# A SwiGLU gate/up projection by seven block products in place of eight, with the sums of weight blocks on GpSimd

## The reference

```python
h = rms_norm(x, ffn_pre_g[l])                      # (512, 1024)
f = silu(h @ w_gate[l]) * (h @ w_up[l])            # w_gate, w_up: (1024, 2816)
f = f @ w_down[l]                                  # w_down: (2816, 1024)
x = x + rms_norm(f, ffn_post_g[l])
```

## Time and profile before

| | us |
|---|---|
| median of 3 runs | 1101.09 (1100.99 to 1101.46) |
| span of the profiled execution | 1098.9 |
| PE busy | 1081.2 |
| DVE busy | 621.1 |
| ACT busy | 410.0 |
| POOL busy | 5.2 |

### The profile page before, as it was taken

One profiled execution on the slowest core, in us unless ns is written; L12 is line 12 of the kernel. 1 busy time (PEld: TensorE's weight loads), 2 busy tenths in 40 slices (PEclk: granted clock), 3 DMA queues, 4 the chain that ended last, 5 costly groups with the idle time before them and its releaser, 6 DMA issues.

```text
span 1098.9 us, 16669 instructions
## 1 busy us (share of the span) xinstructions
PE 1081.2 (98%) x6662; PEld 656.5 (60%) x6662; DVE 621.1 (57%) x1419; ACT 410.0 (37%) x810; POOL 5.2 (0%) x18
## 2 busy tenths in 40 slices
PE   8999999999999999999999999999999999999997
PEld 5887894695444444444488888748744444444443
DVE  6998998973432433322579889898633433422014
ACT  5636355553332332221244464456532322331000
POOL 1000000000000000000000000000000000000000
PEclk9999999999999999999999999999999999999999
DMA  8513212254324323323023150134623323232001
GB/s 310 172 56 102 92 40 97 96 166 142 115 77 153 109 83 115 114 79 115 1 79 115 40 151 5 43 111 154 183 86 115 116 96 115 91 101 77 1 20 58
DMA packets 58173, 109.64 MB, mean 100 GB/s; under 512 B 7025, under 2 KB 7281, under 8 KB 57969
## 3 DMA queue, kind: packets, MB, share of 16 engines
q1 hardware_dynamic: 58096, 108.58, 30.8%
HBM read 106.46 MB, written 2.10 MB: 99 GB/s over the span
## 4 chain that ended last, share of the span: by engine, by line
PE 91%; DMA 3%; DVE 3%; ACT 1%; SPq 1%; issue 1%; ACTq 0%; DVEq 0%
PE ps L508 84%; DMA raw<-weights_dram 3%; PE ps L512 3%; PE ps L716 1%; PE ps L700 1%; DVE ring L1158 1%; DMA xs<-x_dram 1%; DVE E L1287 1%; ACT ring L786 0%; PE ps L635 0%; SPq L453 0%; ACT gbc L786 0%; PE ps L677 0%; PE ps L638 0%; PE ps L620 0%
## 5 line engine op out<-in xcount | busy, mean ns | idle before, releaser
L508 PE MATMUL ps<-hT,ring 128*128 128x512 f16 (+1 forms) x3264 | 547.4, 329 | 0.0
L508 PEld LDWEIGHTS ps<-hT,ring 128*128 128x128 f16 x3264 | 319.1, 98 | 221.4
L508 PE MATMUL ps<-ring,U 128*128 128x512 f16 x1440 | 313.4, 379 | 0.0
L1158 DVE SCALAR_TENSOR_TENSOR ring<-raw,ring 128x512 f16<-128x512 f32 x368 | 231.2, 685 | 89.4 <-ACT ring L786 88.7
L786 ACT ACTIVATE ring<-raw 128x512 f16<-128x512 f32 x368 | 208.1, 621 | 126.6 <-PE ps L508 80.4
L508 PEld LDWEIGHTS ps<-ring,U 128*128 128x128 f16 x1440 | 140.8, 98 | 167.2 <-issue 0.3
L1490 DVE SCALAR_TENSOR_TENSOR R<-ps,R 128x512 f32<-128x512 f32 (+1 forms) x52 | 31.7, 609 | 256.2 <-ACT R L961 255.9
L508 PE MATMUL ps<-ring,hT 128*128 128x256 f16 x1152 | 133.3, 273 | 1.4 <-DVE hT L1247 1.3
L961 ACT ACTIVATE R<-ps 128x512 f32<-128x512 f32 (+1 forms) x52 | 27.6, 530 | 276.1 <-PE ps L508 276.0
L508 PEld LDWEIGHTS ps<-ring,hT 128*128 128x128 f16 x1152 | 112.1, 98 | 16.1 <-issue 1.9
L1287 DVE SCALAR_TENSOR_TENSOR E<-E,par 128x256 f32<-128x256 f32 x240 | 102.1, 479 | 0.2
(11 more groups left out here) (109 smaller groups left out, 498.9 us busy)
## 6 DMA issues: line engine op xcount, KB each, us to landing
raw<-weights_dram SPq DMA_DIRECT2D x368, 256.0 KB, 3.3
gbc<-gains_dram SPq DMA_DIRECT2D x8, 512.0 KB, 6.2
xs<-x_dram SPq DMA_DIRECT2D x4, 512.0 KB, 7.0
U<-weights_dram SPq DMA_DIRECT2D x8, 256.0 KB, 7.9
out_dram<-xs SPq DMA_DIRECT2D x8, 256.0 KB, 2.0
cst<-consts_dram SPq DMA_DIRECT2D x1, 1296.0 KB, 12.2
bd<-pool_w_dram SPq DMA_DIRECT2D x8, 16.0 KB, 9.8
par<-params_dram SPq DMA_DIRECT2D x1, 76.0 KB, 6.7
```

Source lines behind the costliest of these rows:

```text
L508: ins = mm(dst, st, mv_, start=first and i == 0, stop=last and i == 2, **kw)
L1158: V.scalar_tensor_tensor(out=ring[:, slot % RING, 1, raw_part(part)], in0=raw_home(n)[0], scalar=W_SCALE, in1=ring[:, slot % RING, 0, raw_ ...
```

## The change

Gate/up slots 5 to 21 (`FAST`) of each layer, 17 in each, are computed by the Strassen-Winograd scheme. Tokens are cut into halves (256 each), the 1024 rows of the sum into halves (512 each), and the 256 columns into gate and up (128 each). Seven products of 512 rows x 128 columns x 256 tokens take the place of eight. Four of them use sums of weight blocks, four use sums of activation blocks, and three sums of products are needed.

- PE: `seven_products`, 7 x 4 x 3 = 84 matmuls of 256 columns for a slot, in four banks: 0 to 3 or 4 to 7 in turn. Between the products it waits for `p1_copied`, `u_sb`, `c12_ps` and `v_sb`. Two matmuls in each of the first two such slots of a layer set the state of two banks.
- ACT: three copies of 128 x 256 out of PSUM for a slot (`p1_copy`, `u_copy`, `v_copy`); in a layer once, four copies of 128 x 1024 of the transposed activations in float32 (`h32_copy`) and four of their sums to float16 (`hS_hi_of`).
- DVE: two additions of 128 x 256 for a slot (`c12_add`, `c22_add`), both with one operand in PSUM; in a layer once, four sums of 128 x 1024 (`h_sums`) and four low halves of that size (`hS_lo_of`).
- POOL: three additions for a slot, of 128 x 1024, 128 x 512 and 128 x 512 float32, with both operands in SBUF, into `xsum`. Each waits for the one before it. The first waits until DVE has split the third chunk of the FAST slot before, the second until it has split the fourth.
- Splits: a FAST slot has 7 blocks of 128 x 512 in place of 4, split in chunks of 1, 2, 2 and 2 blocks. The last two chunks read `xsum`. `raw` has 8 parts in place of 4. The ring has the same size, but is given out in 32 blocks of 128 x 512 (`QUADS`).
- Order: `hidden_steps` becomes `head_steps` (up to slot 3) and `main_steps`, which spreads the chunks of the next slots between the other steps. In `main_steps` one slot is split for each slot multiplied, but where the slots to split are down slots (4 blocks each) there are two: in layer 0 while f = 19, 20 and 21 run; in layer 1 f = 18 has one FAST and one down slot, f = 19 has one slot, and f = 20 and 21 have two.

```diff
-NRAW = 4
+NRAW = 8
 EARLY = 2 * PARTS
-RING = 8
+QUADS = 32
...
+FAST = tuple(range(GU_HEAD + 1, FT))
...
+        xsum = sb("xsum", [P, 4, RAW])
...
+            for n in FAST_SLOTS:
+                base, i = PARTS * n, 3 * FAST_NO[n]
+                r = (base - EARLY) % NRAW
+                if i:
+                    pool.wait_ge(lo_split, PARTS * FAST_SLOTS[i // 3 - 1] + 3)
+                for part in range(3):
+                    _, landed, value = raw_home(base + part)
+                    pool.wait_ge(landed, value)
+                nc.gpsimd.tensor_tensor(xsum[:, 0:2, :], raw[:, r:r + 2, :], raw[:, r + 1:r + 3, :],
+                                        ALU.add).then_inc(x_sum, 1)
+                if i:
+                    pool.wait_ge(lo_split, PARTS * FAST_SLOTS[i // 3 - 1] + 4)
+                pool.wait_ge(x_sum, i + 1)
+                nc.gpsimd.tensor_tensor(xsum[:, 2, :], xsum[:, 0, :], raw[:, r + 2, :], ALU.add).then_inc(x_sum, 1)
+                _, landed, value = raw_home(base + 3)
+                pool.wait_ge(landed, value)
+                pool.wait_ge(x_sum, i + 2)
+                nc.gpsimd.tensor_tensor(xsum[:, 3, :], xsum[:, 2, :], raw[:, r + 3, :], ALU.add).then_inc(x_sum, 1)
...
+            def seven_products(l, f, between):
+                n, i = l * SLOTS + GU0 + f, fast_no(l, f)
+                ba = gu_bank(f)
+                bb, bc, be = ba + 1, ba + 2, ba + 3
+                for b in (ba, bb, bc, be):
+                    take(b, f_sb, fno(l, f, 0))
+                pe.wait_ge(hS_lo, 4 * (l + 1))
+                if f in FAST[0:2]:
+                    for b in (bb, bc):
+                        mm(bank[b][:, 0:HALF], quad(n, 0, 0)[:, 0:P], hT[:, 0, 0, 0:HALF], start=True, stop=True)
+                def product(b, q, a, first, last):
+                    for k in range(KT // 2):
+                        cols = slice(P * k, P * (k + 1))
+                        for j, (pw, pa) in enumerate(((0, 0), (0, 1), (1, 0))):
+                            ins = mm(bank[b][:, 0:HALF], quad(n, q, pw)[:, cols], a[pa][:, k, :],
+                                     start=first and k == 0 and j == 0, stop=last and k == KT // 2 - 1 and j == 2,
+                                     skip_group_check=True)
+                    return ins
+                def whole(j):
+                    return [hT[:, p, KT // 2 * j:KT // 2 * (j + 1), :] for p in range(2)]
+                def h(i, j):
+                    return [w[:, :, half(i)] for w in whole(j)]
+                def hs_(c):
+                    return [hS[c][:, 0], hS[c][:, 1]]
+                product(ba, Q_A11, h(0, 0), True, True).then_inc(p1_ps, 1)
+                between(2)
+                product(be, Q_X1, hs_(0), True, True)
+                between(4)
+                pe.wait_ge(p1_copied, i)
+                product(bb, Q_X3, hs_(1), False, True).then_inc(p6_ps, 1)
+                between(6)
+                product(ba, Q_B21, h(0, 1), False, True)
+                between(9)
+                pe.wait_ge(u_sb, i)
+                product(bb, Q_X2, hs_(2), False, True).then_inc(p7_ps, 1)
+                between(11)
+                pe.wait_ge(c12_ps, i)
+                product(bc, Q_B22, hs_(3), False, True)
+                between(13)
+                pe.wait_ge(v_sb, i)
+                return product(bb, Q_X4, h(1, 1), False, True)
...
+            def h32_copy(l, t):
+                act.wait_ge(h_lo, xno("fpre", l, t) + 1)
+                copy(h32_by_tile[:, t // 2, :, P * (t % 2):P * (t % 2 + 1)],
+                     pair(t).rearrange("p (k t) -> p k t", k=KT), A_SCALE / RN).then_inc(h32_in, 1)
...
+            def p1_copy(l, f):
+                i = fast_no(l, f)
+                act.wait_ge(p1_ps, i)
+                copy(bank[gu_bank(f) + 1][:, 0:HALF], bank[gu_bank(f)][:, 0:HALF]).then_inc(p1_copied, 1)
+            def u_copy(l, f):
+                i = fast_no(l, f)
+                act.wait_ge(p6_ps, i)
+                if i > 1:
+                    act.wait_ge(c12_ps, i - 1)
+                copy(u_w, bank[gu_bank(f) + 1][:, 0:HALF]).then_inc(u_sb, 1)
+            def v_copy(l, f):
+                i = fast_no(l, f)
+                act.wait_ge(p7_ps, i)
+                if i > 1:
+                    act.wait_ge(c22_ps, i - 1)
+                copy(v_w, bank[gu_bank(f) + 1][:, 0:HALF]).then_inc(v_sb, 1)
...
+            def main_steps(l, i0, i1):
+                for i in range(i0, i1):
+                    f, _ = HIDDEN[i]
+                    new = FREED_BY[l * NU + FIRST_OF[GU0] + i - 1] if i > i0 else []
+                    if i > i0:
+                        silu(l, *HIDDEN[i - 1])
+                    split_hi_chunks(new, 0, 2)
+                    if f in FAST:
+                        p1_copy(l, f)
+                    split_hi_chunks(new, 2, 3)
+                    hidden_hi(l, *HIDDEN[i - 1])
+                    if f in FAST:
+                        u_copy(l, f)
+                    split_hi_chunks(new, 3, 4)
+                    if f in FAST:
+                        v_copy(l, f)
+                silu(l, *HIDDEN[i1 - 1])
+                split_hi(*FREED_BY[l * NU + FIRST_OF[GU0] + i1 - 1])
+                hidden_hi(l, *HIDDEN[i1 - 1])
...
+                elif part == 1:
+                    for j in (1, 2):
+                        _, landed, value = raw_home(i + j)
+                        act.wait_ge(landed, value)
+                    copy(quads2(n, Q_B22, 0), raw_pair(i + 1), W_SCALE).then_inc(hi_split, 1)
+                else:
+                    act.wait_ge(x_sum, 3 * FAST_NO[n] + (1 if part == 2 else 3))
+                    copy(quads2(n, Q_X1 if part == 2 else Q_X3, 0), xsum[:, 2 * part - 4:2 * part - 2, :],
+                         W_SCALE).then_inc(hi_split, 1)
...
+                h32_copy(l, 0)
+                h32_copy(l, 1)
                 split_hi(z + 18)
                 square_y("post", l, 3)
-                hidden_steps(l, 0, 1)
+                head_steps(l, 0, 1)
                 split_hi(z + 19)
                 square_x("fpre", l, 3)
-                split_hi(z + 20)
                 h_hi_of("fpre", l, 2)
+                h32_copy(l, 2)
                 h_hi_of("fpre", l, 3)
-                split_hi(z + 21)
-                hidden_steps(l, 1, len(HIDDEN))
-                hidden_hi(l, *HIDDEN[-1])
-                split_hi(*(z + DN0 + c + RING for c in range(N_DN - DN_TAIL)))
+                h32_copy(l, 3)
+                head_steps(l, 1, 5)
+                for c in range(4):
+                    hS_hi_of(l, c)
+                head_steps(l, 5, 2 * GU_HEAD)
+                main_steps(l, 2 * GU_HEAD, len(HIDDEN))
+                split_hi(*REST[l])
...
+            def c12_add(l, f):
+                b = gu_bank(f)
+                dve.wait_ge(u_sb, fast_no(l, f))
+                V.tensor_tensor(bank[b + 2][:, 0:HALF], bank[b + 3][:, 0:HALF], u_w, ALU.add).then_inc(c12_ps, 1)
+            def c22_add(l, f):
+                b = gu_bank(f)
+                dve.wait_ge(v_sb, fast_no(l, f))
+                V.tensor_tensor(bank[b + 3][:, 0:HALF], bank[b + 3][:, 0:HALF], v_w, ALU.add).then_inc(c22_ps, 1)
...
+            def main_steps(l, i0, i1):
+                for i in range(i0, i1):
+                    f, _ = HIDDEN[i]
+                    new = FREED_BY[l * NU + FIRST_OF[GU0] + i - 1] if i > i0 else []
+                    split_lo_chunks(new, 0, 1)
+                    if i > i0:
+                        hidden(l, *HIDDEN[i - 1])
+                    split_lo_chunks(new, 1, 2)
+                    hidden_lo(l, *HIDDEN[i - 1])
+                    if f in FAST:
+                        c12_add(l, f)
+                    split_lo_chunks(new, 2, 3)
+                    if f in FAST:
+                        c22_add(l, f)
+                    split_lo_chunks(new, 3, 4)
+                hidden(l, *HIDDEN[i1 - 1])
+                split_lo(*FREED_BY[l * NU + FIRST_OF[GU0] + i1 - 1])
+                hidden_lo(l, *HIDDEN[i1 - 1])
...
+                head_steps(l, 1, 4)
+                h_sums(l)
+                head_steps(l, 4, 5)
+                for c in range(4):
+                    hS_lo_of(l, c)
+                head_steps(l, 5, 2 * GU_HEAD)
+                main_steps(l, 2 * GU_HEAD, len(HIDDEN))
+                split_lo(*REST[l])
```

More of the change, by code:

```diff
@@ L105, with fast @@
 assert len(UNIT_AT) == NT * SLOTS
+def fast(n):
+    return n % SLOTS - GU0 in FAST
+QUAD0, BEFORE, holder = [], [], {}
+top = 0
+for n in range(L * SLOTS):
+    if fast(n) and any((top + q) % QUADS == QUADS - 1 for q in (1, 3, 5)):
+        top += 1
+    places = [(top + q) % QUADS for q in range(7 if fast(n) else 4)]
+    QUAD0.append(top)
+    BEFORE.append(max([holder[p] for p in places if p in holder], default=-1))
+    for p in places:
+        holder[p] = n
+    top += len(places)
+FAST_SLOTS = [n for n in range(L * SLOTS) if fast(n)]
+FAST_NO = {n: i for i, n in enumerate(FAST_SLOTS)}
```

(44 more changed lines are left out.)

147 lines of the change are left out of this document (104 added, 43 removed).

## The result

The changed kernel takes **1087.41 us** (median of 4 runs, 1085.18 to 1088.65), the kernel before 1101.28 us beside it: a ratio of 0.9871 [0.9857, 0.9885], 13.9 us faster. Forecast were 1088.8 us in a range of 1066 to 1108. The total was near; three of its terms were far off, one of them too dear and two too cheap. The execution that was profiled is the fastest of the four (1085.18 us): its span of 1083.4 us is 15.5 us under the one before, where the medians differ by 13.9 us.

The account below looks back on a forecast made before the run. The prediction took the changed part to be bound by PE. Its terms, -40.4 + 0.9 + 19.9 + 0.4 + 3.9 + 4 - 1 = -12.3 us, took 1101.1 us to 1088.8 us, range 1066 to 1108 us.

Parts of the forecast that it names:

- the term of the slots: In f = 7 to 18 of each layer, PE waits 0.83 us for `c12_ps` per slot: 24 x 0.83 = +19.9 us.
- the head: Handovers between DVE and POOL in each layer's head make slot 5 start 2 us late: +4 us for two layers.
- the places with two slots at once: Four chunks ahead of `p1_copy` cost 0.6 us in five slots; with f = 18 of layer 1, +3.9 us together.
- 84 matmuls for 48, 34 slots: PE's slot falls from 10.36 to 9.17 us, 1.19 us less in each of 34 slots: -40.4 us.
- `p1_copy` in plain slots: PE's restart after ACT's copy loses between 0 and 0.2 us, taken as 0.1, at f = 5 and 6: +0.4 us.
- eight parts of `raw`: Loads start a slot earlier, so PE loses less to ACT's load waits: between 0 and -5 us, taken as -1.
- The chain: Closed sequence of POOL's sums and DVE's operations setting a FAST slot's period: taken as 10.0 us, between 9.6 and 10.4.
- My table: Timing of one undisturbed FAST slot on ACT and DVE against PE's needs: `c12_add` done by 5.1 us, needed at 6.55.
- half of it lies in the wait already counted: At f = 18 of layer 1, four chunks make `p1_copy` 1.9 us late, half of it inside PE's `c12_ps` wait.
- Rival 1: In slots and head, DVE and POOL don't hold each other up noticeably: 1068.3 us, chance 0.13.
- rival 2: Only POOL waits and DVE always goes first, slot period 9.6 us: 1077 us, chance 0.17.
- Rival 3: Slower: POOL's sums make the slot period exceed 10.5 us, for example 11.2 us and 1118 us; chance 0.20.

Follow-up runs that it names:

- Experiment 4: The changed kernel with DVE's `c12_add` put ahead of `hidden_lo`: 1080.89 us, ratio 0.9818 to the kernel before.
- experiment 5: The changed kernel with one more POOL addition of 128 x 512 in each FAST slot, its result overwritten: 1111.72 us, ratio 1.0101 to the kernel before.
- experiment 3: The changed kernel with POOL's three additions turned into memsets to zero that read nothing: 1063.93 us, ratio 0.9663 to the kernel before.
- 7: The changed kernel with POOL's first sums kept back until the last pre-norm tile is squared, slot 19's split behind that tile: 1085.17 us.
- experiment 8: The changed kernel with only POOL's sum for the second FAST slot kept back until DVE wrote the last pre-norm tile's low half: 1082.06 us.
- 11: The changed kernel with the edits of experiments 4, 6 and 8, and POOL's first sum for the first FAST slot waiting for DVE's slot 18 split: 1063.10 us.
- experiment 2: The changed kernel with POOL's additions cut to the first 128 of each 512 columns: 1064.51 us, ratio 0.9668 to the kernel before.
- Experiment 6: The changed kernel with fewer split chunks ahead of `p1_copy` and DVE's adds where two slots are split at once: 1080.44 us, ratio 0.9813.

## Why the prediction was right, and where it was wrong

The mechanism in the slots was right: DVE and POOL stop each other whole instruction by whole instruction, PE waits for `c12_ps`, and the gain is about a third of what PE's work alone would give. That the total came out within 1.4 us is luck: the term of the slots was 14.6 us too dear, and the head and the places with two slots at once were 13.3 us too cheap. The terms against the span of the profiled execution:

| term | forecast | measured |
|---|---|---|
| 84 matmuls for 48, 34 slots | -40.4 | -40.5 |
| bank state | +0.9 | +0.9 |
| DVE and POOL in turns, in the slots | +19.9 | +5.3 |
| `p1_copy` in plain slots | +0.4 | 0 |
| two slots at once, and f = 18 of layer 1 | +3.9 | +9.3 |
| head | +4 | +11.9 |
| eight parts of `raw` | -1 | -2.3 |
| sum | -12.3 | -15.4 (span 15.5) |

- **The chain was mis-sized.** I took 10.0 us with bounds of 9.6 and 10.4; it is 9.46 us, under both. The list of links was right, in its order too. But I had added up full durations and doubted how much of their fixed part hides. It all hides: a split of 1024 costs 1.08 us after its blocker's end where it takes 1.21 alone, a sum of 512 costs 1.13 where it takes 1.27, `hidden_lo` 0.55 and `c12_add` 0.34. Since PE needs 9.17 us, an error of 0.5 us in 10 made one of 13 us in the time (24 x 0.54): what counts is the distance from the bound, and that is where the precision has to go. Experiment 4 shows the chain from below (without `c12_add` it is 9.12 us, and the loss is zero), experiment 5 from above. The rest of the 14.6 us is the number of slots: I had f = 7 to 18 pay, 24 slots in the two layers, but 17 take 9.47 us and two 9.26 us. My table had `c12_add` in time by 1.4 us; at 0.29 us a slot that lasts for some five slots (an estimate), and the first full wait is at f = 10.
- **The head was mis-sized and misplaced.** I had the start of slot 5 late by 2 us. It was on time; PE waited earlier, for the last pre-norm tile. I had counted DVE's new work and its spare time over the whole head, and not what is queued behind the slot 18 and 19 splits: the statistics of that tile, tiny operations that I had never thought of as something that POOL can hold. Experiments 3, 7, 8 and 11 show it. The clock that falls after such a wait makes it dearer (0.94 in the mean of layer 1's head). So the 4 us stood for a wait that wasn't there.
- **f = 18 of layer 1.** The 1.9 us that I worked out from ACT's queue is there (1.87 us, experiment 3), but "half of it lies in the wait already counted" was wrong: the queue and POOL's third sum are one after the other, and with the lower clock behind them they cost 6.35 us, of which 4.51 us are PE's idle.
- **Two down slots at once**: 0.59 us each, five times; 0.6 forecast.
- **`p1_copy`** has no loss in plain slots (9.17 us exactly). My value was between 0 and 0.2 us.
- The profile was to show splits of up to 3.5 us (3.25) and sums of 2.35 us (2.35, 1.26). ACT was to wait for POOL at the third chunk; it is the fourth (1.41 us), since the third sum is the one that is late.

Rival 1 (nobody waits) falls with the splits of 3.25 us; rival 2 (only POOL waits) too, since a DVE split of 1024 that overlaps a sum ends 1.08 us after it, though the sum of 6.18 us in experiment 2 shows that POOL can wait alone for a while. Rival 3 was near, but not by the period alone: it wanted 10.5 us, and with one sum of 512 more the kernel is slower than before at 10.21 us already, with the head and f = 18 of layer 1.

The rule that I cited (the Trainium skill, SBUF — State Buffer, Who interferes with whom) holds in both directions in these traces: a split of 1.21 us takes 3.25 us behind a sum, and a sum of 1.27 us takes 2.06 us behind a split. By the figure of the Trainium skill's other page (GPSIMD Engine Reference, Elementwise — side-by-side cycle accounting) a slot's three sums would be about 4.5 us, an estimate; undisturbed they take 2.35 + 1.27 + 1.27 = 4.9 us here, as I had estimated.

**What was open: PE's wait for tile 3 in layer 0** is 3.14 us in the kernel after and 3.82 us in that of experiment 4, whose head is the same. The traces show why, first the kernel after, then experiment 4:

```profile
210.47 5.72 DVE L1385 SCALAR_TENSOR_TENSOR ring<-raw,ring 128x512 f16<-128x512 f32 x4
...
211.06 2.91 POOL L557 TENSOR_TENSOR xsum<-raw 128x1024 f32<-128x1024 f32 x1 [194.48 <-DMA raw<-weights_dram]
```

```profile
210.45 6.79 DVE L1385 SCALAR_TENSOR_TENSOR ring<-raw,ring 128x512 f16<-128x512 f32 x4
...
210.76 2.58 POOL L557 TENSOR_TENSOR xsum<-raw 128x1024 f32<-128x1024 f32 x1 [193.80 <-DMA raw<-weights_dram]
```

The load that releases POOL's first sum landed earlier in experiment 4, and the sum began 0.3 us earlier. So it got in behind the first of slot 18's four parts and not behind the second, three parts were held up in place of two, and the split was 1.07 us longer. PE's clock fell after the longer wait too, and the start of slot 5 was about 1.8 us later. Experiment 6 and the kernel of experiment 8 have a split of 6.79 and 6.80 us as well. The profiled execution of the kernel after is thus a lucky one, and the other three (1087.32 to 1088.65 us) may have had the longer form; no trace shows them.

What stays open: whether the 2.0 us left at f = 18 and 19 of layer 1 can be had with earlier loads; it wasn't tried.
